# Building the first expert block's rows on TensorE, joining two stages, and splitting the expert weight loads over two DMA queues

## What is computed

```python
x1 = x + (gate_a * branch_a + gate_b * branch_b) @ w_out
n  = rmsnorm(x1, g_ffn)
g_sel = argmax(n @ w_grp + b_grp)                     # one of 4 groups
e     = top_k((n @ w_exp + b_exp)[group g_sel], 2)    # 2 of its 8 experts
h_e = silu(n @ w_e1[e]) * (n @ w_e3[e])               # 32 experts, hidden width 512
x2 = x1 + sum over the 2 choices of weight * (h_e @ w_e2[e])
```

## Time and profile before

| | |
|---|---|
| median of 3 runs | 1229.91 us (1229.5 to 1231.15) |
| the profiled execution | 1227.32 us |
| its span, first to last instruction | 1225.5 us |
| PE busy | 1084.5 us, 88% |
| VectorE, ScalarE, GpSimd busy | 428.3, 354.5, 391.2 us |
| read from and written to memory | 269.30 MB, 26.54 MB |

### The profile page before, as it was taken

One profiled execution on the slowest core, in us unless ns is written; L12 is line 12 of the kernel. 1 busy time (PEld: TensorE's weight loads), 2 busy tenths in 40 slices (PEclk: granted clock), 3 DMA queues, 4 the chain that ended last, 5 costly groups with the idle time before them and its releaser, 6 DMA issues. The chain is left out here.

```text
span 1225.5 us, 20512 instructions
## 1 busy us (share of the span) xinstructions
PE 1084.5 (88%) x8243; PEld 832.5 (68%) x8243; DVE 428.3 (35%) x988; ACT 354.5 (29%) x748; POOL 391.2 (32%) x428
## 2 busy tenths in 40 slices
PE   5999899899999989999999896888888888887783
PEld 4998898798999877888898673454445444444441
DVE  6698733891111363342323442211211111111116
ACT  6547633352222644453332431000000000000000
POOL 4454458841211443322554101221212112211100
PEclk9999989898988989999999887999999999999996
DMA  7332236255322531114421898999999999999997
GB/s 130 90 83 70 69 83 167 48 158 130 91 74 61 205 103 38 50 53 139 141 79 44 304 425 354 425 428 424 430 425 429 427 429 427 429 427 430 427 427 264
DMA packets 149678, 289.10 MB, mean 236 GB/s; under 512 B 43668, under 2 KB 119028, under 8 KB 132832
## 3 DMA queue, kind: packets, MB, share of 16 engines
q1 hardware_dynamic: 94224, 249.40, 52.4%
q10 hardware_dynamic: 49632, 27.46, 8.3%
q0 software_dynamic: 5744, 11.15, 2.4%
HBM read 269.30 MB, written 26.54 MB: 241 GB/s over the span
## 5 line engine op out<-in xcount | busy, mean ns | idle before, releaser
L492 PE MATMUL bank<-xhi,cv_w_hi 128*128 128x272 f32 x848 | 260.1, 307 | 9.5 <-PEq L135 3.2
L478 POOL TENSOR_TENSOR cv_w_lo<-cv_w_raw,cv_w_hi 128x1024 fp32r<-128x1024 f32 (+1 forms) x69 | 167.9, 2433 | 310.6 <-ACT cv_w_hi L471 291.8
L2559 PE MATMUL bank<-e_w,b_xT 128*64 128x256 f32 x2048 | 231.0, 383 | 24.4 <-DVE b_xT L2588 14.9
L492 PE MATMUL bank<-xhi,cv_w_lo 128*128 128x272 f32 x848 | 251.2, 296 | 0.0
L492 PE MATMUL bank<-xlo,cv_w_hi 128*128 128x272 f32 x848 | 250.4, 295 | 0.0
L2559 PEld LDWEIGHTS bank<-e_w,b_xT 128*64 128x64 f32 x2048 | 147.3, 138 | 98.0 <-DVE b_xT L2588 19.1
L492 PEld LDWEIGHTS bank<-xhi,cv_w_hi 128*128 128x128 f32 x848 | 165.8, 195 | 18.2 <-issue 10.2
L492 PEld LDWEIGHTS bank<-xlo,cv_w_hi 128*128 128x128 f32 x848 | 166.3, 196 | 0.9
L492 PEld LDWEIGHTS bank<-xhi,cv_w_lo 128*128 128x128 f32 x848 | 165.8, 196 | 0.0
L2571 PE MATMUL bank<-e_w,b_hiddenT 128*64 128x512 f32 x512 | 116.9, 598 | 18.9 <-DVE b_hiddenT L2596 18.9
L2524 POOL COPY b_target<-slot_target 128x1 int32 (+1 forms) x31 | 5.5, 178 | 309.0 <-ACT b_y L2581 288.9
(11 more groups left out here) (447 smaller groups left out, 1641.9 us busy)
## 6 DMA issues: line engine op xcount, KB each, us to landing
e_w<-in_w_e SPq DMA_DIRECT2D x96, 2048.0 KB, 32.4
cv_w_raw<-in_w_in ACTq DMA_DIRECT2D x34, 512.0 KB, 4.2
cv_w_raw<-in_w_in SPq DMA_DIRECT2D x18, 512.0 KB, 3.9
cv_w_raw<-in_w_br_b ACTq DMA_DIRECT2D x8, 512.0 KB, 4.1
o_raw<-in_w_out SPq DMA_DIRECT2D x16, 256.0 KB, 3.7
y_rows<-choice_rows SPq DMA_DIRECT2D x8, 512.0 KB, 11.7
g_values_gates<-g_z_stage ACTq DMA_DIRECT2D x12, 272.0 KB, 4.6
f_gates<-g_values_gates SPq DMA_DIRECT2D x2, 1088.0 KB, 8.7
```

The lines of the kernel that those rows point to most:

```text
L478: self.k.nc.gpsimd.tensor_tensor(self.wlo[:, s, 0:nk, :], self.raw[:, s, 0:nk, :], self.whi[:, c % OPS, 0:nk, :].bitcast(F32), ALU.subtract)\
L492: last = self.k.nc.tensor.matmul(self.bank(c, h)[:, 0:HALF], w, x[:, d, cols], start=(d == 0 and n == 0), stop=(d == nk - 1 and n == 2))
L2559: last = nc.tensor.matmul(k.bank[bank][sl[a], 0:FH], xT[:, d, :], w[slot][:, d, FH * a:FH * a + FH], start=(d == 0), stop=(d == KD - 1))
```

## The change

1. **One stage.** `project_and_choose` and `expert_blocks` return five functions each, one for each engine, and `choices_and_experts` runs them one behind the other in a single block. No barrier stands between them.
2. **The first block's rows.** `first_oh` now has a one-hot [rows, 64 slots] for every tile, scaled by the tile's 1/rms. PE's `first_rows(i)` multiplies each tile's residual rows by it, eight matmuls for a tile (128 columns of x against 64), and sums the five tiles in bank 2. This gives the turned rows of the block at once; VectorE copies them to `b_xT` with the gain. The first gather, `place_first`, its addition and block 0's transposes go. The products stand behind `place(3)` and around the last counts; `keep_busy` goes. VectorE makes three more small instructions for each tile.
3. **The residual rows stay in SBUF.** The stores `keep_p`, `keep_s` and the reload `x_back` go. For that the ring of w_e2 has 3 slots. w_e1 and w_e3 have a fourth slot, which only block 3 uses: later blocks take slots (b-1) mod 3. The fourth w_e3 slot holds the router's small tiles until the choice is made, so its load waits for `normed` and `picked`.
4. **w_e2 from ScalarE's queue.** From expert 3 on, w_e2 of expert b+3 is issued by ScalarE behind its eviction of block b. w_e1 and w_e3 stay on SyncE's queue.
5. **Smaller things.** Silu and product share one tile; the sample rows' `c_xn` has a buffer of its own; three gather buffers instead of two; the loop is written out for 7 blocks and rolled by 3; `dynamic_dma_scratch_size` is 4096 instead of 8192.

```diff
-RING = 4
-PAIRS = 2
+RING = 3
+EARLY = 7
...
-            k.run(project_and_choose)
-            k.routing.close()
-            k.run(expert_blocks)
+            k.run(choices_and_experts)
...
-            sp.wait_ge(added1, 2)
-            sp.dma_start(k.keep_p[:, 0:2, :], k.x[:, 1:3, :]).then_inc(k.x_kept, 16)
...
-            sp.wait_ge(added1, 5)
-            sp.dma_start(k.keep_s, k.x[0:NS, 0, :]).then_inc(k.x_kept, 16)
+        sp.wait_ge(k.normed, 5)
+        sp.wait_ge(k.picked, 1)
+        load_weights(k, sp, "w_e3", k.w3, k.w3_loaded, 3, 3)
...
+        def first_rows(i):
+            t, n = tiles[i][1], tiles[i][3]
+            pe.wait_ge(columns, i + 1)
+            for d in range(KD):
+                last = nc.tensor.matmul(TA[:, SLOTS * d:SLOTS * d + SLOTS], k.x[0:n, t, :].rearrange("n (p k) -> n k p", k=KD)[:, d, :],
+                                        k.first_oh[0:n, t, :], start=(i == 0 and d == 0), stop=(i == 4 and d == KD - 1))
+            if i == 4:
+                last.then_inc(k.turned, 1)
...
+        place(3, tiles[3][3])
+        first_rows(0)
+        first_rows(1)
+        count(4, tiles[4][3])
+        pe.wait_ge(chosen, 6)
+        nc.tensor.matmul(L[1][:, 0:NE], k.ones[:], run[:, 1, :], start=True, stop=True).then_inc(counted, 1)
+        for i in range(2, 5):
+            first_rows(i)
+        place(4, tiles[4][3])
...
+            v.wait_ge(ranked, i + 1)
+            V.tensor_scalar(scaled[0:n, :], k.oh[0:n, 0, t, 0:1], rr[0:n, t:t + 1], None, ALU.mult)
+            c(V.tensor_scalar(other[0:n, :], r1[1][0:n, 0:SLOTS], k.oh[0:n, 1, t, 0:1], rr[0:n, t:t + 1], ALU.mult, ALU.mult))
+            V.scalar_tensor_tensor(out=k.first_oh[0:n, t, :], in0=r1[0][0:n, 0:SLOTS], scalar=scaled[0:n, :], in1=other[0:n, :],
+                                   op0=ALU.mult, op1=ALU.add).then_inc(columns, 1)
...
+        ranks(4)
+        v.wait_ge(k.turned, 1)
+        v.wait_ge(k.last_tabled, 16)
+        for a in range(2):
+            f = slice(4 * a, 4 * a + 4)
+            V.tensor_tensor(k.xT[:, f], TA[:, 4 * SLOTS * a:4 * SLOTS * a + 4 * SLOTS].rearrange("p (k s) -> p k s", k=4),
+                            k.gain[:, f].unsqueeze(2).broadcast_to([128, 4, SLOTS]), ALU.mult).then_inc(k.copied, 1)
+        v.wait_ge(listed, 5)
...
+        V.tensor_copy(k.total[:], L[1][:, 0:NE]).then_inc(k.picked, 1)
...
-        def loads(sp, e, b, slot, prev):
-            sp.wait_ge(first, prev + 1)
-            load_weights(k, sp, "w_e1", k.w1, k.w1_loaded, e, slot)
-            sp.wait_ge(up, prev + 1)
-            load_weights(k, sp, "w_e3", k.w3, k.w3_loaded, e, slot)
-            sp.wait_ge(down, prev + 1)
-            load_down(k, sp, e, slot)
+    def loads_up(sp, e, prev, u):
+        sp.wait_ge(first, prev + 1)
+        load_weights(k, sp, "w_e1", k.w1, k.w1_loaded, e, u)
+        sp.wait_ge(up, prev + 1)
+        load_weights(k, sp, "w_e3", k.w3, k.w3_loaded, e, u)
...
+    def scalar_with_load(a, b, u, nu, d2, nd, half, m):
+        scalar_part(a, b, u, nu, d2, nd, half, m)
+        load_down(k, a, b + RING, d2)
...
+        for b in range(RING + 1, EARLY):
+            loads_up(sp, b, b - RING - 1, (b - 1) % RING)
+        with sp.Fori(EARLY // RING, LAST // RING) as i:
+            for s in range(RING):
+                b = RING * i + s + 1
+                loads_up(sp, b, b - RING, s)
+        loads_up(sp, NE - 1, NE - 1 - RING, (NE - 2) % RING)
...
-            eng.wait_ge(up, NE - 2)
-            eng.dma_start(xr[:, 1:5, :], k.keep_p).then_inc(x_back, 16)
-            eng.dma_start(xr[0:NS, 0, :], k.keep_s).then_inc(x_back, 16)
             eng.wait_ge(all_in, 1)
...
-    nc = _bacc.Bacc("TRN2", target_bir_lowering=False, num_devices=1, dynamic_dma_scratch_size=8192)
+    nc = _bacc.Bacc("TRN2", target_bir_lowering=False, num_devices=1, dynamic_dma_scratch_size=4096)
```

More of the change, by code:

```diff
@@ L2451, in expert_blocks @@
+    return on_sync, on_gpsimd, on_scalar, on_tensor, on_vector
 def expert_blocks(k):
@@ new lines, in expert_blocks @@
+    last_oh = k.over("m_last_oh", [128, 5, 2 * SLOTS], F32, "c_xn")
+    last_rows = k.over("m_last_rows", [128, 5, 128], F32, "e_w1_1")
+    nothing = k.over("b_nothing", [128, D // 2], F32, "c_xn", 2 * D)
+    ohw = T("last_weight", 2, 5)
+    other = k.over("m_other", [128, 2 * SLOTS], F32, "c_xn", past)
+    b1 = k.over("m_blk_oh", [128, 10, MORE], F32, "c_xn", past)
+    cmpj, ejf = k.over("m_cmpj", [128, MORE, NE], F32, "c_xn"), T("ejf", MORE)
+    names = ("index", "first", "up", "silu", "hidden", "hturned", "hcopied", "down", "out")
@@ new lines, in expert_blocks @@
+    turned, copied = k.turned, k.copied
+    index, first, up, silu, hidden, hturned, hcopied, down, out = (k.sem("b_" + n) for n in names)
+    aimed, targets, diffs, exps, coded, listed, planned, all_in, added, summed = (k.sem("m_" + n) for n in (
+        "aimed", "targets", "diffs", "exps", "coded", "listed", "planned", "all_in", "added", "summed"))
+    blank, blanked, last_made, last_turned, last_kept, last_in, finished = (k.sem("m_" + n) for n in (
+        "blank", "blanked", "last_made", "last_turned", "last_kept", "last_in", "finished"))
@@ L2584, in vector_part, with scalar_part @@
+    def scalar_part(a, b, u, nu, d2, nd, half, m):
+        a.wait_ge(first, b + 1)
+        wait(a, hturned, b)
+        nc.scalar.activation(hm[:], k.bank[1][:, 0:FH], ACT.Silu).then_inc(silu, 1)
+        a.wait_ge(down, b + 1)
+        wait(a, stored, 16 * b)
+        nc.scalar.activation(y[:], k.bank[4][:], ACT.Copy).then_inc(out, 1)
+    def vector_part(v, b, u, nu, d2, nd, half, m):
+        if half is not None:
             v.wait_ge(turned, b + 1)
@@ new lines, in expert_blocks, with load_rows @@
+    yrows = k.over("y_rows", [128, 5, 2, D], F32, "late", 6 * KD * FE)
+    whole = k.ytok.rearrange("(m two) n -> m (two n)", two=2)
+    def load_rows(eng):
+        eng.wait_ge(all_in, 1)
+        for m, t in enumerate(ORDER):
+            for j in range(2):
+                c0, rows = NT * j + ROW0[t], TILES[t][1]
+                eng.dma_start(yrows[0:rows, t, j, :], whole[c0:c0 + rows, :]).then_inc(k.got[2 * m + j], 16)
+    END = [k.bank[5:7], [k.bank[7], k.bank[0]], k.bank[1:3], k.bank[3:5], k.bank[5:7]]
```

1156 lines of the change are left out of this document (553 added, 603 removed).

## The result

| | before | after |
|---|---|---|
| median | 1229.43 us (8 runs) | 1239.84 us (8 runs) |
| ratio to before, 95% interval | | 1.0086 (1.0063 to 1.0109) |
| span of the profiled execution | 1225.5 us | 1234.3 us |
| mean granted clock | 0.956 | 0.953 |

The changed kernel is 0.86% slower, 10.6 us of 1229. The forecast was 1229.5 us with a range to 1235.5, and it lies outside.

The account below looks back on a forecast made before the run. The prediction took reading the expert weights at 427 GB/s as the bound. Block 30 ending 6.4 us later nearly cancelled the faster reload and additions: -0.4 us on the profiled span, forecast 1229.5 us, range 1223 to 1235.5.

Parts of the forecast that it names:

- The first block comes earlier, by 7.2 us: Front of the expert stage: first up product at 744.8 us instead of 751.99, after PE's one-hot products and counts.
- Rival (D): Front: clock stays low under the 64-column first_rows products, first block at 748.8, +3.6 to +5.2 us, slower; chance 0.12.
- Rival (E): Front: a store, copy or other wait holds the first block near 752, so the change does not take hold; slower, chance 0.03.
- X follows the first block 1:1: Weight stream: the last weight's landing, X, moves as the first block does, to 1193.1 us; the stream starts 1.7 us earlier.
- The residual reload, 5.5 us: End of the kernel: without the reload, all_in to VectorE's first addition falls from 9.64 to 4.1 us, a gain of 5.5.
- Two queues: Last blocks: queues alternate by packet, block 31's three matrices land together, and block 30 ends at 1189.8 us, 6.4 later.
- rival (C): Last weights: w_e2 gets ahead, block 30 ends at 1192.3 us, +2.1 us, kernel at 1232.0; chance 0.13.
- Third gather buffer: gathers never ended a wait of PE; nothing: Expert blocks: three gather buffers instead of two were expected to change nothing.
- What a second issuer saves: Weight loads: transfers of all issuers interleave on the same engines, so issuing w_e2 from ScalarE saves only issue time: nothing.
- Rival (B): Expert blocks: w_e2 falls behind its third of the rate, block 30 ends at 1200.5; +10.3 us, 1240.2, slower; chance 0.08.

Follow-up runs that it names:

- the kernel with wide products and the scatter first: Changed kernel with 512 residual-row columns moving in the one-hot products, and GpSimd's scatter before its wait for the gather's landing; ratio to before 0.9990.

## Why the prediction was wrong

**"The first block comes earlier, by 7.2 us": this step failed.** It priced `first_rows` at 0.27 us a matmul, the price of L2306, on the ground that both load 128x128 weights. Measured: 0.49. On M's scale the first block came 2.9 us later than before, a miss of 10 us. The bound for it, 748.8, took everything at 1.45 times, from a stretch with the clock at 0.66; the clock was 0.50, and the columns 32 bytes apart would have kept the price there at the full clock too. Both reasons are shown, by the two runs that took each away alone. The factor 1.45 itself was read from two rows of L2323 with different shapes (128 rows in the stretch at 0.66, 32 rows later), so it was not a price of the clock alone.

A rule that would have spoken against the price stands in the Trainium skill (SBUF — State Buffer, section Door 1: The DMA port swizzle): SBUF is read in lines of 16 bytes, and every access that goes to a new line pays. The prediction did not weigh it. For the stationary operand this case agrees in direction: 335 ns with every element in a line of its own, 192 ns with four to a line, both at the full clock. That the lines are the mechanism no run here shows.

**Rival (D), the clock stays low.** It happened (0.50 from 730 to 755), had 0.12, and was priced too low. Its first block at 748.8 was one factor on a price that had two. Rival (E) put the first block near 752, where it came, but expected a wait as the cause, and PE was busy throughout 730 to 755.

**"X follows the first block 1:1": right in kind, wrong from the wrong start.** w_e3 of 3 was issued 26.9 us into M against 18.7 before: 8.2 us later instead of 1.7 earlier. With one queue the last eviction is 480.5 us into M (1207.11 less 726.64) against 469.9: +10.6. That leaves 2.4 us beyond the 8.2. About 1.3 of them are visible: the queue runs short of work just before w_e1 of 7 is issued, at 812.58 in the kernel with w_e2 on SyncE's queue. It is the place where block 3 frees no up slot, and where the prediction had the two limits coincide. The windows of that kernel, and then of the kernel before:

```profile
806.00:808.00 2.00, 2.00 (x17) 0.73 (x13) 0.00 (x0) 0.32 (x1) 0.00 (x0) 1.00 0.91 381
808.00:810.00 2.00, 1.48 (x16) 0.96 (x15) 0.76 (x2) 0.28 (x1) 0.96 (x3) 1.00 0.83 205
```

```profile
806.00:808.00 2.00, 1.48 (x17) 0.79 (x15) 0.76 (x2) 0.60 (x1) 0.36 (x2) 1.00 1.09 463
808.00:810.00 2.00, 2.00 (x22) 1.33 (x20) 0.00 (x0) 0.00 (x0) 1.40 (x3) 1.00 0.98 422
```

Of the last 1 us I can't show the owner; that w_e2 of 3 now waits for block 0's down product is a candidate.

**The residual reload, 5.5 us: right in the profile.** all_in to the first addition fell from 9.64 to 4.4 us, 5.2. Putting 2 MB back costs 4.5 in the profile. The time that it gives is a little less, 2.7 to 3.6 us, and not clear of noise.

**"Two queues": near in size, and only partly in mechanism.** The +6.4 us for block 30 contain the 1.7 by which X was to come earlier; by themselves the queues had +8.1. Taking them away gave 6.6. The prediction's mechanism (the last matrices land in step, and a block is computed behind them) fits what remains when GpSimd's wait is taken out: in the kernel with wide products and the scatter first, block 30 ends some 3 us before the last weight lands, between the two ends that the prediction weighed (5.8 and 0.8), with w_e2 slightly ahead, as rival (C) had it. What it missed is the gather.

**"Third gather buffer: gathers never ended a wait of PE; nothing": this sentence failed.** It asked only PE. The gather ended a wait of GpSimd, and behind that stood the scatter, the eviction and the next silu. Three numbers give it: 8.5 us of landing and 3.2 of copies and issues are 11.7 us, less than PE's 13.5; 11.7 and 3.2 are 14.9, more. The term belonged to the two queues, not to the buffer. In the kernel before with two queues it is worth 12 us. In the changed kernel it is worth between nothing (by the ratio) and 4 us (by M, and beside the wide products); this is not settled more closely. One reading, argued and not shown: three matrices take 14.7 us at 427 GB/s, as long as GpSimd's step, so the weights hold the blocks to nearly the same period once GpSimd no longer does.

**What a second issuer saves.** The prediction cited the Trainium skill (DMA: Bandwidth & Descriptors, Issuing engines are not separate DMA queues), that a second issuer saves only issue time. The runs agree that it gave no bandwidth (427 GB/s both ways) and add that it was not free: 0.54% here.

**Rival (B)** has the time that came out, 1240.2, and is wrong all the same: PE never waited for w_e2, and q10 emptied before q1. A right number is no evidence for its story.

The sum: up to the last eviction +10.6 with one queue (about 8.2 of it the late start of w_e3, 1.3 the short supply near 808, 1 without an owner), reload and additions -5.9 (last eviction to the end of the span, 26.8 before and 20.9 with one queue), two queues +6.6. That these make +11.3 us, the whole of M, is no check, since all are differences of the same three profiles; each rests on its own run. The prediction had -1.7, -5.5 and +8.1, and -1.3 of small ones (landings, waits between the additions), in all -0.4. Of the miss of 11.7 us, 9.9 are the start of w_e3 and 2.4 the stream behind it; the others are 1.5 us and less, and nearly cancel.

## What to carry to other kernels

Take the price of a matmul from one whose weights lie as its own will: same stride, same clock. Where one operand must be read with a stride and the other is narrow, make the narrow one the weights and let the wide one move. And before a transfer queue is added beside a small, latency-bound transfer that some engine waits for, add up that engine's own step (landing and issues) and compare it with the period of the engine that is thought to be the bound.

## What the runs showed of the hardware

- A 128x128 f32 weight load took 192 ns with neighbouring columns at the full clock, 335 ns with columns 32 bytes apart at the full clock, and 333 to 335 ns at the half clock either way. The products with 64 moving columns took 0.49 us with both against them, 0.48 with the stride alone, 0.44 with the half clock alone.
- The same strided columns as the moving operand, 512 wide, made the whole of that work in 9.75 us instead of 19.7 (at a granted clock of 0.67 and then 1.00, against 0.50).
- The granted clock fell to 0.50 and stayed there for 25 us with PE busy throughout, on products of 64 columns; with 512 columns in the same place it was 0.67 in 735 to 740 and 1.00 in 740 to 745.
- A second weight queue lengthened a gather's landing from 8.5 (8.1 with one queue in the new layout) to 11.7 us and a scatter's from 7.8 to 9.4, at the same total rate.
- Up to the issue at which M begins the kernels took between 722 and 734 us, a spread of 1% of the whole, with nearly the same code. A gain of 0.3% in a profile is lost in that unless it is counted from a common event.
